# Four output tiles instead of three follow each normalised tile behind the first layer's output norms, and the third weight chunk is split between and behind them

## What is computed

```python
def rms_norm(x, g):
    return x * rsqrt(mean(x * x, axis=-1) + 1e-6) * g

# first layer (layer 0)
h = rms_norm(x, pre_mix_norm)
mix = hybrid_mixer(h, w_in, ...)                 # recurrence, gated attention, block attention
x = x + rms_norm(mix @ w_out, post_mix_norm)     # first output norm
h = rms_norm(x, pre_ffn_norm)
f = (silu(h @ w_ffn_gate) * (h @ w_ffn_up)) @ w_ffn_down     # 1024 -> 2816 -> 1024
x = x + rms_norm(f, post_ffn_norm)               # second output norm
# second layer (layer 1), likewise the third (layer 2)
h = rms_norm(x, attn_norm_g)
p = h @ w_in                                     # and so on, without output norms
```

## Time and profile before

| | |
|---|---|
| time, median of 3 runs | 1020.79 us (1020.69 to 1020.94) |
| the profiled execution: its time, its span | 1020.92 us, 1019.1 us |
| TensorE, matmuls busy | 1001.6 us (98%) |
| VectorE busy | 683.8 us (67%) |
| ScalarE busy | 503.0 us (49%) |
| GpSimd busy | 3.0 us |
| DMA, mean over the span | 153 GB/s, queue of weights 40.9% busy |
| granted TensorE clock, mean | 0.999 of full speed |

### The profile page before, as it was taken

How to read it: one execution, slowest core, us unless ns; L and a number is a source line. 1 busy time by engine, 2 the same in 40 slices (tenths; PEclk the granted TensorE clock), 3 DMA queues, 4 the chain that set the end, 5 groups by cost and what they waited for, 6 DMA issues and landing times.

```text
span 1019.1 us, 20189 instructions
## 1 busy us (share of the span) xinstructions
PE 1001.6 (98%) x8766; PEld 950.1 (93%) x8766; DVE 683.8 (67%) x1089; ACT 503.0 (49%) x663; POOL 3.0 (0%) x8
## 2 busy tenths in 40 slices
PE   9999999999999999999999999999999999999997
PEld 8898989999999888879999999999887899999997
DVE  6868576776555887865665555588967576555555
ACT  6476664344444653554644343465536364444433
POOL 0000000000000000000000000000000000000000
PEclk9999999999999999999999999999999999999999
DMA  9435435454544232222555454543221254554531
GB/s 331 177 116 196 142 133 198 169 206 167 194 179 155 89 114 105 85 77 106 183 193 204 166 203 170 186 159 107 92 95 74 78 208 170 175 197 168 204 125 42
DMA packets 24024, 156.41 MB, mean 153 GB/s; under 512 B 2608, under 2 KB 3936, under 8 KB 6400
## 3 DMA queue, kind: packets, MB, share of 16 engines
q1 hardware_dynamic: 21888, 151.70, 40.9%
q10 hardware_dynamic: 1840, 2.50, 0.7%
q0 software_dynamic: 208, 0.92, 0.3%
HBM read 154.05 MB, written 1.06 MB: 152 GB/s over the span
## 4 chain that ended last, share of the span: by engine, by line
PE 86%; DVE 7%; ACT 4%; issue 2%; DMA 1%; SPq 0%; ACTq 0%; DVEq 0%
PE bank L464 72%; DVE w_lo L1639 2%; ACT w_hi L1185 2%; DVE arena L1621 1%; PE bank L899 1%; DVE x L1621 1%; PE bank L904 1%; PE bank L915 1%; DMA x<-in_x 1%; ACT h_hi L1218 1%; PE bank L1123 1%; DVE h_lo L1694 1%; PE bank L1153 1%; DVE arena L2100 1%; DVE h_lo L1646 0%
## 5 line engine op out<-in xcount | busy, mean ns | idle before, releaser
L464 PE MATMUL bank<-h_hi,w_hi 128*128 128x256 f32 x1480 | 425.6, 288 | 6.0 <-DVE w_lo L1639 3.1
L1639 DVE TENSOR_TENSOR w_lo<-raw,w_hi 128x2048 fp32r<-128x2048 f32 (+3 forms) x144 | 323.1, 2250 | 156.1 <-ACT w_hi L1185 155.4
L464 PE MATMUL bank<-h_lo,w_hi 128*128 128x256 f32 x1480 | 418.6, 283 | 0.0
L464 PE MATMUL bank<-h_hi,w_lo 128*128 128x256 f32 x1480 | 418.5, 283 | 0.0
L1185 ACT ACTIVATE w_hi<-raw 128x2048 fp32r<-128x2048 f32 (+1 forms) x145 | 270.0, 1867 | 78.7 <-PE bank L464 77.1
L464 PEld LDWEIGHTS bank<-h_hi,w_hi 128*128 128x128 f32 x1480 | 283.4, 192 | 16.8 <-DVE h_lo L1694 4.6
L464 PEld LDWEIGHTS bank<-h_lo,w_hi 128*128 128x128 f32 x1480 | 283.6, 192 | 0.9 <-issue 0.7
L464 PEld LDWEIGHTS bank<-h_hi,w_lo 128*128 128x128 f32 x1480 | 283.6, 192 | 0.0
L464 PE MATMUL bank<-mix_hi,w_hi 128*128 128x256 f32 x720 | 207.0, 288 | 2.2 <-DVE mix_lo L1621 1.4
L464 PE MATMUL bank<-mix_lo,w_hi 128*128 128x256 f32 x720 | 203.7, 283 | 0.0
L464 PE MATMUL bank<-mix_hi,w_lo 128*128 128x256 f32 x720 | 203.7, 283 | 0.0
(11 more groups left out here) (305 smaller groups left out, 844.0 us busy)
## 6 DMA issues: line engine op xcount, KB each, us to landing
raw<-in_w SPq DMA_DIRECT2D x136, 1024.0 KB, 4.8
raw<-in_w SPq DMA_DIRECT2D x5, 512.0 KB, 3.7
raw<-in_w SPq DMA_DIRECT2D x2, 896.0 KB, 4.5
raw<-in_w SPq DMA_DIRECT2D x2, 768.0 KB, 4.1
cst<-in_consts SPq DMA_DIRECT2D x1, 1184.0 KB, 10.4
arena<-bias_rows ACTq DMA_DIRECT2D x1, 1024.0 KB, 7.6
out<-arena ACTq DMA_DIRECT2D x4, 256.0 KB, 2.1
mat<-in_mat POOLq DMA_DIRECT2D x2, 384.0 KB, 3.4
```

The source lines that it names most:

```text
L464: last = pe.matmul(dst, w[a](k), act[b](k), start=start and i == 0 and j == 0, stop=stop and i == n - 1 and j == 2, skip_group_check=loose)
L1639: dve.tensor_tensor(w_lo[:, s, 0:n], raw[:, s, 0:n], w_hi[:, s, 0:n].bitcast(F32), ALU.subtract)\
```

## The change

At both places of layer 0 (and nowhere else):

- `as_they_come` follows each tile with four output tiles instead of three: all of chunk 1 goes along, and nothing of it is left for behind the last tile. The second entry of `pieces` gets the mark that releases chunk 1.
- Chunk 2's hi part is made in four quarter copies on ScalarE, one behind each of the tiles 2 to 5 (`hi_quarter`), instead of one copy behind `square`. Its lo part is made in two halves on VectorE directly behind the last tile (`lo_in_halves`), ahead of `square_sum`, and TensorE takes its first output tile in two halves to match (`first_product`). The count `lo_dve` grows by two for such a chunk, hence the new `n_lo`.
- The next norm's sum on TensorE stands behind chunk 2's first output tile instead of in front of chunk 2.
- ScalarE's table load ahead of the next norm's factor is dropped. The table of Ln and Exp is then still the one loaded for the output norm.
- In the output norms VectorE adds the last two part sums as well (`part` 3) and TensorE has one matmul with ones fewer. In the second place VectorE makes lo of chunk 1 ahead of the part sums, and TensorE takes both of ScalarE's late squares before the part sum.
- In the feed-forward part VectorE's `gu` 0 goes ahead of lo of chunk 4.

```diff
-        n_lo = [n + 2 for n in range(NCH)]
+        HALVED = (CHUNK[0, "gu", 2], CHUNK[1, "in", 2])
+        n_lo = [n + 2 + sum(h <= n for h in HALVED) for n in range(NCH)]
...
+            def first_product(dst, c, at):
+                pe.wait_ge(lo_dve, n_lo[c] - 1)
+                product(dst, tile_of(c, KT, 2 * P, at), range(KT // 2), H, stop=False, loose=True)
+                split(pe, c)
+                product(dst, tile_of(c, KT, 2 * P, at), range(KT // 2, KT), H, start=False, loose=True)
...
             # norm_sum, output norms
                 pe.matmul(bank[into][:, 0:T], ONES, sq[:, 6, :], start=True, stop=False)
-                pe.wait_ge(V.sem, V.at(l, what, "part", 2))
+                if what == "fed":
+                    pe.wait_ge(A.sem, A.at(l, what, "sq", 7))
+                    pe.matmul(bank[into][:, 0:T], ONES, sq[:, 7, :], start=False, stop=False)
+                    pe.wait_ge(V.sem, V.at(l, what, "part", 3))
+                    pe.matmul(bank[into][:, 0:T], ONES, sq[:, 0, :], start=False, stop=True)\
+                        .then_inc(M.sem, M.mark(l, what, "sum"))
+                    return
+                pe.wait_ge(V.sem, V.at(l, what, "part", 2 if what == "final" else 3))
                 pe.matmul(bank[into][:, 0:T], ONES, sq[:, 0, :], start=False, stop=False)
-                pe.matmul(bank[into][:, 0:T], ONES, sq[:, 1, :], start=False, stop=False)
+                if what == "final":
+                    pe.matmul(bank[into][:, 0:T], ONES, sq[:, 1, :], start=False, stop=False)
...
             # first_projections (layer 1; ffn likewise for layer 0)
-                pieces = [(1, projected(l, 0), columns_of(l, 0)), (0, projected(l, 1), columns_of(l, 1)[:1])]
+                pieces = [(1, projected(l, 0), columns_of(l, 0)), (2, projected(l, 1), columns_of(l, 1))]
                 as_they_come(l, "in", pieces[:2 if l == 1 else 1])
-                project(l, 1, begun=(l == 1))
+                if l != 1:
+                    project(l, 1)
...
             # gate_up (project likewise)
-                        if not (begun and t == 0):
+                        if c in HALVED and t == 0:
+                            first_product(gate_up_bank(j)[:, t, :], c, 0)
+                        else:
                             last = product(gate_up_bank(j)[:, t, :], tile_of(c, KT, 2 * P, t * P), range(KT), H)
-                        if l and j == 1 and t == 0:
+                        if (j, t) == (1 if l else 2, 0):
                             norm_sum(l, "ffn")
-                    if l == 0 and j == 1:
-                        norm_sum(l, "ffn")
...
             # ScalarE
+            def hi_quarter(c, n):
+                if n == 0:
+                    act.wait_ge(loaded[c % RING], 16 * (c // RING + 1))
+                    act.wait_ge(M.sem, released(c - RING))
+                part = slice(n * CH // 4, (n + 1) * CH // 4)
+                last = copy(w_hi[:, c % RING, part], raw[:, c % RING, part])
+                if n == 3:
+                    last.then_inc(hi_act, 1)
...
                                 .then_inc(A.sem, A.mark(l, what, "hi", k))
+                            if 2 <= k < 6:
+                                hi_quarter(CHUNK[l, "gu" if what == "ffn" else "in", 2], k - 2)
...
-                if what in ("in", "ffn"):
+                if what in ("in", "ffn") and (l, what) not in BY_TILE[1:]:
                     ln_and_exp()
...
             # VectorE
+            def lo_in_halves(c):
+                dve.wait_ge(hi_act, n_hi[c])
+                for part in (slice(0, CH // 2), slice(CH // 2, CH)):
+                    dve.tensor_tensor(w_lo[:, c % RING, part], raw[:, c % RING, part],
+                                      w_hi[:, c % RING, part].bitcast(F32), ALU.subtract).then_inc(lo_dve, 1)
...
                 part_sum(l, what, 2)
+                after_v(l, what, "part", 2)
+                tt(sq[:, 0, :], sq[:, 0, :], sq[:, 1, :], ALU.add, l, what, "part", 3)
...
             # normed_residual
-                part_sums(l, what)
+                if what == "mixed":
+                    part_sums(l, what)
                 lo_of(chunk)
+                if what == "fed":
+                    part_sums(l, what)
...
                 lo_of_tile(KT - 1)
+                lo_in_halves(chunk + 1)
...
             # ffn
-                def feed(j):
+                def scaled(j):
                     after_m(l, "gu", j)
...
                     tt(FF["gu"][:, j % 2, :, :], gate_up_bank(j), wide(rstd[:, :], 2), ALU.mult, l, "gu", j)
+                def feed(j):
+                    if j or l:
+                        scaled(j)
...
                 after_a(l, "ffn", "rstd")
+                if l == 0:
+                    scaled(0)
                 after(CHUNK[l, "gu", 1])
```

More of the change, by code:

```diff
@@ L541, in first_projections, with project @@
                 last.then_inc(M.sem, M.mark(l, "in", "rstd"))
-            def project(l, *which, begun=False, between=lambda: None):
+            def project(l, *which, between=lambda: None):
                 for i in which:
@@ L547, in project @@
                     width = STREAM[c][3] // KT
-                    split(pe, c)
+                    if c not in HALVED:
+                        split(pe, c)
                     to = projected(l, i)
@@ L565, in project @@
                                 between()
-                            if not (begun and t == 0):
+                            if c in HALVED and t == 0:
+                                first_product(to[:, t, :], c, at)
+                            else:
                                 last = product(to[:, t, :], tile_of(c, KT, width, at), range(KT), H)
-                            if (l, i, t) in ((0, 1, 0), (2, 1, 0)):
+                            if (l, i, t) in ((0, 1, 0), (1, 2, 0), (2, 1, 0)):
                                 norm_sum(l, "in")
                     last.then_inc(M.sem, M.mark(l, "in", i))
-                    if (l, i) == (1, 1):
-                        norm_sum(l, "in")
             def turn(l, j):
@@ L604, in ffn, with gate_up @@
             def ffn(l):
-                def gate_up(j, begun=False):
+                def gate_up(j):
                     c = CHUNK[l, "gu", j]
-                    split(pe, c)
+                    if c not in HALVED:
+                        split(pe, c)
                     if j >= 3:
@@ L655, in ffn @@
                 pieces = [(1, gate_up_bank(0), [(c, 2 * P, 0), (c, 2 * P, P)]),
-                          (0, gate_up_bank(1), [(c + 1, 2 * P, 0)])]
+                          (2, gate_up_bank(1), [(c + 1, 2 * P, 0), (c + 1, 2 * P, P)])]
                 as_they_come(l, "ffn", pieces[:2 if l == 0 else 1])
-                gate_up(1, begun=(l == 0))
+                if l:
+                    gate_up(1)
                 for p in range(1, FT // 2):
@@ L1553, in _ @@
                 else:
-                    hi_of(CHUNK[l, "in", 2])
+                    if l == 2:
+                        hi_of(CHUNK[l, "in", 2])
                     hi_of(CHUNK[l, "in", 3])
@@ L1586, in _ @@
                 square(l, "ffn")
-                hi_of(c0 + 2)
+                if l:
+                    hi_of(c0 + 2)
                 ffn(l)
@@ L2294, in _ @@
                 square_sum(l, "ffn")
-                lo_of(c0 + 2)
+                if l:
+                    lo_of(c0 + 2)
                 ffn(l)
@@ L2299, in _ @@
                     square_sum(l + 1, "in")
-                    lo_of(CHUNK[l + 1, "in", 2])
                     lo_of(CHUNK[l + 1, "in", 3])
```

## The result

The changed kernel takes **1013.96 us** (median of 4 runs, 1013.86 to 1014.16) against 1020.87 (4 runs, 1020.69 to 1021.10) for the kernel before on the same chip: a ratio of 0.9931, 95% interval 0.9919 to 0.9944. The forecast was 1013.7. The profiled execution took 1013.86 us, its span is 1012.1 us at a mean granted clock of 0.999. The time axis of this trace starts 0.13 us later in the program, so that a place untouched by the change reads 0.13 less here than in the rows of before.

What follows compares the result with a forecast made beforehand. TensorE, its matmuls busy 98% of the span, bounds the kernel, so only its waits can give time back. Gains of 4.4 and 2.7 us at the two places sum to 7.1, giving 1013.7 us, range 1012.2 to 1015.2.

Steps and rivals of the forecast that it cites:

- Norm matmuls, 0.43 and 0.41: Output norms at both places: one fewer on TensorE's chain gains 0.43 us at the first place, 0.41 at the second.
- Four outputs per tile leave no hole, and met waits cost nothing: Tiles, first place: 12 matmuls take 1.44 us against a 1.40 period, so no holes; waits met in advance priced at nothing.
- The rival of met waits: Tiles, first place: each wait met in advance still costs TensorE 0.11 us, 0.9 in all, giving 1014.6 us; chance 0.14.
- Quarter copies fit into ScalarE's idle time: ScalarE between tiles: each copy, 0.42 to 0.63 us, fits in 0.89 us idle, so tiles aren't held up.
- The norm sum is asked for 0.2 later than `square_sum` ends: First place, behind chunk 2's first output: VectorE's squares are summed 0.2 us before TensorE needs them; the tightest meeting.
- `gu` 0 must come ahead of chunk 4's lo, or 3 us are lost: First place, ahead of chunk 3: with this evacuation as late as before, TensorE would wait and lose 3 us.
- The halves: Chunk 2's lo on VectorE, first place: two instructions of 1.23 us, one right behind the other, so TensorE doesn't wait.
- the flush rule: VectorE: a pipe flush behind every instruction would stretch chunk 2's two lo instructions about 1 us each; 1017.4 us, chance 0.03.
- Dropped table load, worth nothing: ScalarE ahead of the next norm's factor, first place: saving 1.28 us gains nothing, as ScalarE waits for the sum then.
- 1.0 us of slack left at chunk 7: Feed-forward part: of the least slack, 3.0 us, 2.0 goes and one is left, so the gain lasts to the second place.
- The rival that the part gives back: Feed-forward part: ScalarE and VectorE lose over 1 us, TensorE stops at chunk 7; up to 2 us, 1014 to 1015.7; chance 0.10.
- Second place: TensorE waits 1.5 for `in` 1, VectorE's wait at the scan gives up 0.9: Ahead of `project(l, 3)`: TensorE idles 1.5 us for the evacuation; VectorE needs 0.9 of its 2.31 wait; gain 2.7.

## Why the prediction was right, point by point

- *Norm matmuls, 0.43 and 0.41.* Right: 0.78 for both when they are put back.
- *Four outputs per tile leave no hole, and met waits cost nothing.* Right: 120 matmuls in 14.65 us. At 0.120 apart they are 14.4, and the rest is the long first matmul and the end of the last. The rival of met waits (0.14) is out. Taken back, the fourth output costs 4.1 us.
- *Quarter copies fit into ScalarE's idle time.* Right: 0.61 each, 0.36 left, and the tiles still 1.40 apart (VectorE's lo's). One whole copy costs 2.9.
- *The norm sum is asked for 0.2 later than `square_sum` ends.* Right in order: it ran at 143.69 with no wait. But the forecast called this only the tightest meeting and set no price on missing it by much; the run with the norm sum in front lost 5.75, some 4 of it by the waits.
- *`gu` 0 must come ahead of chunk 4's lo, or 3 us are lost.* Right as a wait (3.04) and too small as a price: 5.0 at the median, since the clock fell behind the idle time. The text had no row on what an idle TensorE costs beyond its idle time.
- *The halves.* The forecast built chunk 2's start on them and weighed the flush rule against them. The rows were rightly preferred to the rule: two halves took 2.35 us where one takes 1.23. The Trainium skill (VectorE: DVE Perf Modes, The DRAIN you can't avoid) also says, in the paragraph that the forecast drew on, that an instruction which isn't held starts earlier; these two agree with that sentence. But the halves as such carry only 0.3 to 0.5 of the 6.9 us. This the forecast did not work out, and it was there to be had: a whole lo ends at 141.27 on its axis, TensorE's tiles at 140.99.
- *Dropped table load, worth nothing.* The profile agrees: ScalarE waits 2.05 for the norm sum over that time, longer than the load's 1.28. It was not put back by itself.
- *1.0 us of slack left at chunk 7.* Right, 0.9 in the trace: delays of 1.26 and 2.5 cost 0.44 and 1.93. The rival that the part gives back is out: TensorE never waits there, and 0.9 was left.
- *Second place: TensorE waits 1.5 for `in` 1, VectorE's wait at the scan gives up 0.9.* Right: 1.47, and 0.84. That the wait is the shift standing ahead of the evacuation is shown by the run that swaps them.
- *Sum 7.1.* The profiled executions differ by 7.06, the medians by 6.91; 4.4 and 2.7 by place against 4.51 and 2.47 in the runs of one place alone.

## What to carry to other kernels

Fill a stall only after asking which hand-over is next in line: here four outputs per tile and the earlier chunk were worth their 6.9 us only together with the place of two small instructions, the norm sum and `gu` 0, that stood in other queues. Either of them put back took 5.0 to 5.75 us away. Where two engines run ahead of a third in a loop, compare the loop's period (6.15) with the third's (5.76) and count the chunks until the lead is gone, instead of reading busy shares. And price a wait on TensorE by more than its length. Here those of 2.58 and 3.04 us cost clock besides, those up to 1.47 did not, and no length between was tried. Where such a wait can't be avoided, products that nothing reads can fill it: that took the 3.04 us wait's loss from 5.0 to 3.1 us.

## What was not expected of the hardware

- An idle stretch of 3.04 us on TensorE was followed by 6.0 us at a granted clock of 0.51, with the fall within the stretch. One of 2.58 was followed by 3.3 us at 0.50, with the fall some 1.5 us behind its end and matmuls at full speed between. One of 2.61 in the same run was followed by no fall, nor was any of 1.47 and less. By its times the same kernel was hit in some runs and spared in others (1017.2 to 1019.9), while every kernel without such a wait kept within 0.9 us. Twelve passes of idle products took the effect away.
- A wait between 256-column matmuls costs 0.26 to 0.27 us beyond the idle time that the timeline shows: 0.88 of waits made 1.41 in the run with one whole copy, 2.61 made 2.88 with the norm sum in front, and 0.21 made 0.48 with a whole lo. In the first it was a third of the loss at that place.
